# Gate and branch weights in a three-slot ring: loads exchanged, branch weights loaded in halves

## What is computed

```python
gates = jax.nn.sigmoid((proj[..., OFF_MEMQ:] + b_gate).astype(jnp.float32)).astype(x.dtype)
gates = gates.reshape(B, S, N_BRANCH, D_MODEL)
merged = (gates[:, :, 0] * (y_mla @ w_br_mla)
          + gates[:, :, 1] * (y_dil @ w_br_dil)
          + gates[:, :, 2] * (y_mem @ w_br_mem))
x = x + _rms_norm(merged @ w_o, g_post_mix)
h2 = _rms_norm(x, g_pre_ffn)
x = x + _rms_norm(_conv_ffn(h2, w_ffn_up, conv_w, conv_b, w_ffn_down), g_post_ffn)
```

## Time and profile before

| | us |
|---|---|
| median of 3 runs | 3266.5 |
| lowest, highest | 3265.04, 3266.86 |
| the profiled execution | 3263.36 |
| its span in the trace | 3261.5 |
| TensorE (PE) matmul busy in the span | 2970.4 (91%) |
| VectorE busy | 1322.7 (41%) |
| ScalarE busy | 976.0 (30%) |

### The profile page before, as it was taken

One profiled execution on the slowest core, in us unless ns is written; L12 is line 12 of the kernel. 1 busy time (PEld: TensorE's weight loads), 2 busy tenths in 40 slices (PEclk: granted clock), 3 DMA queues, 4 the chain that ended last, 5 costly groups with the idle time before them and its releaser, 6 DMA issues.

```text
span 3261.5 us, 38098 instructions
## 1 busy us (share of the span) xinstructions
PE 2970.4 (91%) x15878; PEld 1879.8 (58%) x15878; DVE 1322.7 (41%) x2814; ACT 976.0 (30%) x2457; POOL 64.7 (2%) x52
## 2 busy tenths in 40 slices
PE   7799999999999769979999789999898888799998
PEld 3567777778777555645554335464554433488743
DVE  3357475575665534322222233322243210577501
ACT  1335546356454430012232222212233301211101
POOL 0000000000000000000000000000000000000000
PEclk9899999999999889999999999999999999899999
DMA  5101101101012027101000120111111012122111
GB/s 201 40 10 55 44 21 45 55 20 41 20 44 80 20 88 296 52 33 52 26 26 33 35 90 26 52 61 69 65 52 77 4 74 107 48 83 98 54 71 44
DMA packets 76508, 196.78 MB, mean 60 GB/s; under 512 B 56144, under 2 KB 61008, under 8 KB 64944
## 3 DMA queue, kind: packets, MB, share of 16 engines
q1 hardware_dynamic: 49648, 172.48, 14.3%
q10 hardware_dynamic: 26688, 21.86, 2.1%
HBM read 182.79 MB, written 11.53 MB: 60 GB/s over the span
## 4 chain that ended last, share of the span: by engine, by line
PE 79%; DVE 9%; ACT 6%; DMA 4%; issue 1%; ACTq 0%; SPq 0%; DVEq 0%
PE ps L968 13%; PE ps L1649 8%; PE ps L1061 5%; PE ps L1586 5%; PE ps L1464 5%; PE ps L1281 3%; PE ps L1596 3%; PE ps L1468 2%; PE ps L1024 2%; ACT arena L1686 2%; PE ps L1348 2%; PE ps L958 2%; PE ps L1363 2%; PE ps L1282 2%; ACT arena L1687 2%; DVE arena L2388 2%
## 5 line engine op out<-in xcount | busy, mean ns | idle before, releaser
L1686 ACT ACTIVATE arena<-ps 64x64 f32<-64x64 f32 (+8 forms) x952 | 313.8, 358 | 1013.8 <-PE ps L968 355.1
L968 PE MATMUL ps<-arena 128*128 128x512 f32 (+1 forms) x976 | 421.2, 591 | 46.1 <-DVE arena L2277 15.2
L968 PEld LDWEIGHTS ps<-arena 128*128 128x128 f32 x976 | 188.0, 194 | 273.4 <-issue 229.8
L1024 PE MATMUL ps<-arena 128*128 128x512 f32 x512 | 264.7, 598 | 1.7 <-DVE arena L2277 1.7
L1649 PE MATMUL ps<-arena 128*128 128x256 f32 x1176 | 254.5, 378 | 0.0
L1649 PEld LDWEIGHTS ps<-arena 128*128 128x128 f32 x1176 | 222.3, 189 | 32.5 <-issue 0.5
L1586 PE MATMUL ps<-arena 128*128 128x512 f32 x384 | 173.5, 604 | 20.0 <-issue 20.0
L1464 PE MATMUL ps<-arena 128*128 128x512 f32 x384 | 179.8, 596 | 5.1 <-ACT arena L2033 3.1
L1687 ACT ACTIVATE arena<-ps,arena 128x128 f32<-128x128 f32 x544 | 156.7, 380 | 84.5 <-PE ps L1179 43.3
L1061 PE MATMUL ps<-arena 128*128 128x256 f32 x768 | 180.3, 388 | 0.0
L1025 PEld LDWEIGHTS ps<-arena 128*128 128x128 f32 x512 | 97.0, 189 | 124.6 <-issue 124.6
(11 more groups left out here) (295 smaller groups left out, 4152.1 us busy)
## 6 DMA issues: line engine op xcount, KB each, us to landing
arena<-in_ada_w SPq DMA_DIRECT2D x12, 2048.0 KB, 17.0
arena<-in_w_up SPq DMA_DIRECT2D x11, 2048.0 KB, 7.7
arena<-in_w_dil SPq DMA_DIRECT2D x9, 2048.0 KB, 7.5
arena<-in_w_dn SPq DMA_DIRECT2D x8, 2048.0 KB, 10.4
arena<-in_w_gate SPq DMA_DIRECT2D x6, 2048.0 KB, 12.3
arena<-in_w_down SPq DMA_DIRECT2D x8, 1408.0 KB, 5.9
arena<-in_att_in SPq DMA_DIRECT2D x5, 2048.0 KB, 7.7
arena<-in_w_z SPq DMA_DIRECT2D x8, 1024.0 KB, 4.9
```

Of the source, the lines that this page charges most:

```text
L968: m = e.matmul(out, w[:, (k * m_tiles + x) * 128:(k * m_tiles + x) * 128 + 128], src(k), start=k == 0, stop=k == nk - 1)
L1024: e.matmul(ps[:, b1, :], w, uT[:, k * T_ALL + 256:(k + 1) * T_ALL], start=k == 0, stop=k == 7)
L1686: return e.activation(out, x, ACT.Copy)
```

## The change

The loads `br 1` and `gate 2` exchange places in the list, and so do `br 2` and `gate 4`; the slots stay as they were. The branch weights are laid out in device memory so that the first half of a row holds what the first four output blocks need, and the second half the rest. For `br 1` and `br 2`, `fetch` issues the first half (1 MB) after the fourth branch product of the branch before, under a semaphore of its own (`br_half`), and the second half after the eighth. `w_o 0` and `w_o 1` exchange slots 0 and 1. On TensorE the wait for the branch weights moves out of `gate` into `branch_`, where the first four products of branches 1 and 2 wait for the first half and the other four for the whole; the offset of the weights in the slot follows the new layout. The sizes, the number of matmuls and the work of the other engines are the same.

```diff
         for br in range(3):
-            load("br", br, ("branch_pe", br, 7), D["w_br"][br])
+            load("br", br, ("branch_pe", br, 7), *([D["w_br"][br, :, 0:2048], D["w_br"][br, :, 2048:]] if br else [D["w_br"][br]]))
...
+        at_load = {x[:2]: i for i, x in enumerate(LOADS)}
+        for br in (1, 2):
+            i = at_load["br", br]
+            LOADS[i], LOADS[i + 1] = LOADS[i + 1], LOADS[i]
+        SLOT_OF["w_o", 0], SLOT_OF["w_o", 1] = SLOT_OF["w_o", 1], SLOT_OF["w_o", 0]
...
-                if s in held:
+                if s in held and not (name == "br" and n):
                     e.wait_ge(*at(*USED[held[s]]))
...
                 a = 0
+                if name == "br" and n:
+                    e.wait_ge(*at("branch_pe", n - 1, 3))
+                    e.dma_start(ring[s][:, 0:2048], parts[0]).then_inc(*landed("br_half", n))
+                    e.wait_ge(*at("branch_pe", n - 1, 7))
+                    a, parts = 2048, parts[1:]
...
             def gate(br, n):
                 b, w = 4 + 2 * (n % 2), slab("gate", 2 * br + n // 4)
                 x = n % 4
-                e.wait_ge(*here("br", br))
                 e.wait_ge(*here("gate", 2 * br + n // 4))
...
             def branch_(br, n):
                 b, w = 5 + 2 * (n % 2), slab("br", br)
-                y = (y_mla, y_dil, y_mem)[br]
+                y, a = (y_mla, y_dil, y_mem)[br], n // 4 * 2048 + n % 4 * 128
+                e.wait_ge(*(at("br_half", br) if br and n < 4 else here("br", br)))
...
-                    m = e.matmul(ps[:, b, :], w[:, k * 1024 + n * 128:k * 1024 + n * 128 + 128], y[:, k * 512:(k + 1) * 512],
+                    m = e.matmul(ps[:, b, :], w[:, a + k * 512:a + k * 512 + 128], y[:, k * 512:(k + 1) * 512],
...
-    D["w_br"] = np.stack([_tiles(a[n][0], 1024)[0] for n in ("w_br_mla_2", "w_br_dil_2", "w_br_mem_2")])
+    D["w_br"] = np.stack([np.concatenate(_tiles(a[n][0], 512), 1) for n in ("w_br_mla_2", "w_br_dil_2", "w_br_mem_2")])
```

## The result

| | before | changed |
|---|---|---|
| median | 3266.68 us (4 runs) | 3236.97 us (4 runs) |
| lowest, highest | 3265.04, 3267.01 | 3235.45, 3238.22 |
| profiled execution | 3263.36 | 3235.73 |
| its span | 3261.5 | 3233.9 |

The ratio is 0.9908, with a 95% interval from 0.9896 to 0.992. I had predicted 3235, between 3228 and 3242.

A forecast was written before the change was run, and what follows sets the result against it. TensorE, busy 91% of the span, was taken as the bound, time being won where it stands still or runs at half clock. 7.4 + 1.2 + 12.9 + 2.1 + 6.2 + 1.9 = 31.7 us off 3266.5 gave 3235, range 3228 to 3242.

The forecast's parts named there:

- The cause of the waits: Ahead of the first gates of branches 1 and 2: TensorE waits for the gate's own load, 20.0 us together.
- Place 1: First gate of branch 1: starts at about 2486.0 rather than 2493.42, 7.4 us, plus 1.2 us of clock.
- The clock term: First gate of branch 1: less of it runs at slow clock, gain between 0 and 2.37, taken as 1.2 us.
- Place 2: First gate of branch 2: starts without a wait, 12.9 us, and takes 7.04 instead of 9.14, 2.1 us.
- That sentence of the prediction: Ahead of the first gate of branch 2: TensorE waits 2.12 us and keeps full clock, so the gate gains 2.1 us.
- the rival on the clock: First gates and output products: waits go but the clock is not given back; gain 28.6, time 3238, chance 0.10.
- Place 3: Output products: start at about 2706.6 instead of 2712.79, 6.2 us, and run at full clock, 1.9 us.
- The covers: New loads land before use: gate 4 and half of br 2, issued about 2535, some 65 us ahead.
- no row's chain took over place 1: Rival at Place 1: a later row's latency takes back the gain; gain 23.1, time 3243, chance 0.04.
- the queue did issue early: Rival in the SyncE queue: early loads are still held by a wait; time 3266.5, chance 0.03.
- the clock was not cut in the longer run without pause: Rival from 2484 through the output products: clock cut over some 255 us without rest; time some 3275, chance 0.02.

The follow-up runs named there:

- e2_wait_only: Kernel before with only the wait for the branch weights moved from the gate product into the branch product, loads as before: 3266.05 us, ratio 1.0002.
- e1_slots: Kernel before with only the slots of the output weights exchanged: 3258.99 us, ratio 0.9978.
- e3_whole: Changed kernel without the halves, branch weights of branches 1 and 2 loaded whole after the eighth branch product: 3239.75 us, ratio 0.9921.
- e10_one_step: Changed kernel with e6_late_sum and e7_recip_first edits, first gate of branch 1 behind the first scores, each later product in its predecessor's place: 3218.03 us, ratio 0.9856.
- e6_late_sum: Changed kernel with TensorE's wait for the last sum moved to the eighth contraction step of each output product, which reads it: 3233.48 us.
- e7_recip_first: Changed kernel with VectorE taking branch 1's multiply and add after the next row's reciprocals instead of ahead of them: 3228.79 us.
- e11_shifted: Changed kernel with four contraction steps of gate(1, 1) computed twice, 3.4 us more TensorE work: 3239.97 us, one run.
- e4_halves: Kernel before with only the branch weights loaded in halves, no exchange of loads or slots: 3260.71 us, ratio 0.9989.
- e12_half_shift: Changed kernel with two contraction steps of gate(1, 1) computed twice, 1.7 us more TensorE work: 3238.79 us, one run.

## Why the prediction was right, step by step

- **The cause of the waits** was read rightly from issue and landing (e2_wait_only), against what the chain of the trace named.
- **Place 1**: start of the gate 7.5 us earlier relative to the scores, for 7.4 worked out. The clock term was 1.4 us (7.98 instead of 9.41), between its bounds, where I took 1.2.
- **Place 2**: the wait of 12.73 us went and the gate took 7.04 us, 15.0 as predicted. But I had taken the clock of 1.00 after the wait of 2.12 us over from the earlier trace rows, and in the changed kernel it fell there: 1.7 us lost. That sentence of the prediction is the step that failed, and its size is why 30.2 came out for 31.7 (1.7 us lost here, 0.3 won at place 1). The same sentence served as evidence against the rival on the clock; it was weak evidence, since one wait at one moment doesn't speak for another.
- **Place 3**: a start 1.5 us after the last branch product and 55.31 us for the products, 8.0 us for 8.1 (e1_slots alone gives the same 8.0). Here the short wait did leave the clock up.
- **The halves** I had costed only by their cover. They turned out to be worth nearly nothing, 1 us (e3_whole); the prediction never asked what the change would be without them.
- **The covers held**: no wait for `br_half`, for slot 0 ahead of a branch product, or for the later `up` loads. One of them was misread. The product at 2531.18 in the earlier trace rows is the third branch product of branch 1; the fourth starts at 2545.01 in the same timeline and ends near 2548.6, so `gate 4` and the half of `br 2` were due 14 us later than the 2535 of the prediction. In the changed kernel the half is issued at 2543.08, still some 60 us ahead of the gate at 2603.14, so nothing hung on it. Matmuls beside the new transfers kept their pace, as the stretch in which `gate 2` and most of the half of `br 1` arrive shows (issued at 2436.94 and 2437.31, landed 7.3 and 10.7 us later):

```profile
2434.00:2447.00 13.00, 13.00 (x49) 7.22 (x48) 7.53 (x11) 5.15 (x7) 0.00 (x0) 1.00 0.63 242
```

- **The rivals**: no row's chain took over place 1; the queue did issue early; the clock was not cut in the longer run without pause (granted clock 1.00 from 2603 to 2682 and from 2690 to 2743).
- **The medians** moved by 29.7 us, the stretch by 30.2. I can't divide the rest between scatter and a cause: the profiled execution before lay 3.3 us under its median and the changed one 1.2.

## What to carry to other kernels

When an in-order queue feeds a ring of slots, ask of each load when its own slot came free and when it was issued: a load that stands behind one whose slot is let go later is late for no reason of its own, and exchanging two pairs of list entries and one pair of slot numbers, with the wait moved to the product that needs it, was worth 29 of 30 us here (e3_whole), and the slot numbers alone 8 (e1_slots). To learn which of several loads a wait is for, add issue and landing times rather than trust the name in the bracket. Once an early load has freed a product from its wait, use it: put it where another chain's latency has no cover (e10_one_step), and give each product the place that the one before it had.

## What the runs showed of the hardware

Behind the same wait of TensorE, 2.12 us long, the granted clock fell to 1.2 GHz in five kernels (the changed one, e3_whole, e6_late_sum, e7_recip_first, e11_shifted) and stayed at 2.4 GHz in five (the kernel before, e1_slots, e2_wait_only, e4_halves, e12_half_shift), with one profiled execution each. In e12_half_shift the only difference from the changed kernel was 1.7 us more work ahead of the wait. A fall there cost 1.7 us, and it came only after the product behind the wait had begun. The clock fell behind none of the waits of 1.5 us ahead of the output products, which took 55.31 us each time. And each wait of 1.48 us in the memory attention cost 1.74 us from start to start (four of them, 7.0 us, e7_recip_first).
